# RWKV recurrence on one core: sixteen adaptive-norm row sums move from the turns of head pairs to the two draining turns and the state loop

## The reference

```
mod = silu(c) @ ada_w[i] + ada_b[i]                       # 6 * 1024 numbers
sh1, sc1, g1, sh2, sc2, g2 = split(mod)
h = rms(x) * (1 + sc1) + sh1
y = rwkv7_mix(h)          # scan over time: state = state * w + (state a) b + v k ; y = state r ; 16 heads of 64
x = x + g1 * y
h = rms(x) * (1 + sc2) + sh2                               # before the feed-forward
x = x + g2 * swiglu(h)
```

## Time and profile before

| | us |
|---|---|
| median of 3 runs | 2743.61 |
| lowest and highest run | 2742.07, 2745.13 |
| the profiled execution | 2749.12 |
| its span, first to last instruction | 2747.3 |
| PE busy in the span | 2567.3 (93%) |
| DVE busy in the span | 1184.1 (43%) |

### The profile page before, as it was taken

One profiled execution on the slowest core, in us unless ns is written; L12 is line 12 of the kernel. 1 busy time (PEld: TensorE's weight loads), 2 busy tenths in 40 slices (PEclk: granted clock), 3 DMA queues, 4 the chain that ended last, 5 costly groups with the idle time before them and its releaser, 6 DMA issues.

```text
span 2747.3 us, 33836 instructions
## 1 busy us (share of the span) xinstructions
PE 2567.3 (93%) x14040; PEld 1977.9 (72%) x14040; DVE 1184.1 (43%) x1813; ACT 978.5 (36%) x1441; POOL 977.9 (36%) x338
## 2 busy tenths in 40 slices
PE   7996667899999999999999999989899999999899
PEld 6745565388887878878887778969587777666586
DVE  4565884664444262442113352434306424444504
ACT  4652443432322243533232332222324334433423
POOL 2312320644444433453444444414433433222232
PEclk8997897899999999999999999999999999999999
DMA  6121343215555322122224332212122222111121
GB/s 263 62 77 42 91 91 118 79 69 191 193 188 199 138 92 77 47 77 77 92 94 171 133 126 92 95 42 95 39 92 86 87 88 96 62 48 61 39 92 62
DMA packets 92101, 272.11 MB, mean 99 GB/s; under 512 B 54720, under 2 KB 54848, under 8 KB 64320
## 3 DMA queue, kind: packets, MB, share of 16 engines
q1 hardware_dynamic: 89232, 255.03, 26.4%
q10 hardware_dynamic: 2736, 15.21, 1.4%
HBM read 264.44 MB, written 5.78 MB: 98 GB/s over the span
## 4 chain that ended last, share of the span: by engine, by line
PE 82%; DVE 8%; ACT 4%; issue 2%; DMA 2%; POOL 2%; SPq 0%; ACTq 0%; POOLq 0%; DVEq 0%
PE bank L348 20%; PE bank L350 20%; PE bank L349 20%; PE bank L284 2%; PE bank L283 2%; PE bank L282 2%; PE bank L2745 1%; PE bank L3279 1%; POOL ring_low L379 1%; PE bank L3257 1%; PE bank L2991 1%; DVE probs L3469 1%; ACT w_high L369 1%; PE bank L809 1%; PE bank L3261 1%
## 5 line engine op out<-in xcount | busy, mean ns | idle before, releaser
L379 POOL TENSOR_TENSOR ring_low<-ring,w_high 128x2048 fp32r<-128x2048 f32 (+2 forms) x184 | 803.3, 4367 | 1324.2 <-ACT w_high L369 1324.2
L348 PE MATMUL bank<-h_high,w_high 128*128 128x512 f32 (+1 forms) x1304 | 519.0, 398 | 7.5 <-POOL ring_low L379 3.6
L350 PE MATMUL bank<-h_high,ring_low 128*128 128x512 f32 (+1 forms) x1304 | 516.8, 396 | 0.0
L349 PE MATMUL bank<-h_low,w_high 128*128 128x512 f32 (+1 forms) x1304 | 513.7, 394 | 0.0
L369 ACT ACTIVATE w_high<-ring 128x2048 fp32r<-128x2048 f32 (+2 forms) x184 | 331.0, 1801 | 359.9 <-PE bank L350 341.2
L348 PEld LDWEIGHTS bank<-h_high,w_high 128*128 128x128 f32 (+1 forms) x1304 | 244.6, 188 | 70.1 <-issue 6.8
L349 PEld LDWEIGHTS bank<-h_low,w_high 128*128 128x128 f32 (+1 forms) x1304 | 244.3, 187 | 60.1 <-issue 0.7
L350 PEld LDWEIGHTS bank<-h_high,ring_low 128*128 128x128 f32 (+1 forms) x1304 | 244.4, 187 | 59.4
L348 PE MATMUL bank<-z_high,w_high 128*128 128x512 f32 x384 | 154.3, 402 | 6.1 <-DVE z_low L3476 2.7
L350 PE MATMUL bank<-z_high,ring_low 128*128 128x512 f32 x384 | 153.5, 400 | 0.0
L349 PE MATMUL bank<-z_low,w_high 128*128 128x512 f32 x384 | 153.0, 398 | 0.0
(11 more groups left out here) (451 smaller groups left out, 4436.2 us busy)
## 6 DMA issues: line engine op xcount, KB each, us to landing
ring<-in_stream SPq DMA_DIRECT2D x194, 1024.0 KB, 4.8
ada_slot<-in_ada_next SPq DMA_DIRECT2D x40, 512.0 KB, 3.3
ada_slot<-in_first SPq DMA_DIRECT2D x8, 1024.0 KB, 5.4
gain_weights<-in_gains ACTq DMA_DIRECT2D x4, 2048.0 KB, 12.2
scale_weights<-in_first SPq DMA_DIRECT2D x4, 1024.0 KB, 19.2
inverse<-scratch_inverse SPq DMA_DIRECT2D x16, 256.0 KB, 4.2
w_first<-in_first SPq DMA_DIRECT2D x2, 1024.0 KB, 8.1
x_res<-in_x SPq DMA_DIRECT2D x2, 1024.0 KB, 12.4
```

Source lines behind the costliest of these rows:

```text
L348: pe.matmul(out, w_high[:, k, cols], x_high, start=start, stop=False)
L349: pe.matmul(out, w_high[:, k, cols], x_low, start=False, stop=False)
L350: return pe.matmul(out, w_low[:, k, cols], x_high, start=False, stop=stop)
L379: pool.tensor_tensor(self.c.ring_low[:, b % SLOTS, 0:cols], self.c.ring[:, b % SLOTS, 0:cols], self.high_buf[:, b % 2, 0:cols].bitcast(F32 ...
```

## The change

`next_ada` leaves the 8 turns `0 <= p < KD`. The same eight calls now stand: `next_ada(0)` at the end of turn 8, `next_ada(1)` and `next_ada(2)` at the end of turn 9, and `next_ada(3)` to `next_ada(7)` in the steps c = 1 to 5 of the state loop, each behind the four state operations. SP issues the eight 1 MB loads no longer one a turn, but in a row behind the last of the four `g1` rows, each behind the sums of the one before. The loads of weight blocks for `rwkv_output` now wait for the last of the sums.

```
@@ vector, turns @@
-            if solves:
-                next_ada(p)
             if p == KD:
                 bonus_tile(1, 4)
                 g1_row(1)
...
                 bonus_tile(2, 0)
                 g1_row(2)
                 g1_row(3)
+                next_ada(0)
+            if p == KD + 1:
+                next_ada(1)
+                next_ada(2)
@@ vector, state loop @@
                 dve.tensor_tensor(part(new, g), part(Tm, g), decay_of(g, c), ALU.mult).then_inc(state.sem, 1)
+            if c <= 5:
+                next_ada(2 + c)
             if c == 1:
                 gated_tile(3, 4)
@@ sync, turn(p) @@
-            if p:
-                ada_sum.wait(sp, p - 1)
-            sp.dma_start(ada_slot[:, :], chip.io["first"][6 + p]).then_inc(ada_in.sem, 16)
@@ sync, behind the turns @@
         chip.load(sp, b_g)
-        ada_sum.wait(sp, KD - 1)
         for n in range(2):
             if n:
                 g1_sum.wait(sp, 1)
             sp.dma_start(g1_slot[:, :, :], chip.io["gains"][0, 0, 0, :, 2 * n:2 * n + 2, :]).then_inc(g1_in.sem, 16)
+        g1_sum.wait(sp, 3)
+        for n in range(KD):
+            if n:
+                ada_sum.wait(sp, n - 1)
+            sp.dma_start(ada_slot[:, :], chip.io["first"][6 + n]).then_inc(ada_in.sem, 16)
         y1_out.wait(sp, KD - 1)
-        g1_sum.wait(sp, 3)
+        ada_sum.wait(sp, KD - 1)
```

## The result

| | before | changed |
|---|---|---|
| median of 5 runs, us | 2745.13 | 2770.38 |
| lowest and highest, us | 2742.07, 2748.65 | 2763.83, 2776.43 |
| the profiled execution, us | 2749.12 | 2768.57 |
| its span, us | 2747.3 | 2766.8 |

The ratio is 1.0093, with a 95% interval of 1.0070 to 1.0115: the change costs 25.3 us by the medians. The forecast was 27.8 us and 2771.4.

The account below looks back on a forecast made before the run. PE, busy 93% of the span, was taken as the bound, so DVE changes count only where PE waits. Terms 28.8 + 1.5 + 0.5 - 3.0 = +27.8 us on 2743.6 gave 2771.4 us, range 2763 to 2780.

Parts of the forecast that it names:

- the ring of load and tiles: State loop: one load and two tiles alternate, 0.1 issue + 5.4 landing + 2.4 tiles = 7.9 us a step.
- the merge held up by the first load: Drain: DVE waits for load 0 and does two tiles ahead of the last y2 merge, which comes 8.0 us later.
- The turns, -3.0: Turns 0 to 7 without tiles and loads: 3.0 us given back, bounds 0 and 6.3.
- The drain, +16.3: From the last g1 row through three tile pairs: bonus_tile(3) starts at 500.7 instead of 484.36, 16.3 us later.
- rival 3: PE's clock falls in longer gaps: +9 us, 2780.5, in the loop; a part, +2.5, in the results part. Chance 12%.
- The loop, to +29.5 at the last state: State loop: with steps of 7.9 us the last state ends at 542.15 against 512.67, 29.5 us later.
- The landing term: In each loop step, the time a load takes to land after issue: 5.4 us.
- the tile term: In each loop step, the time of two tiles: 2.4 us, at 1.22 each.
- Meeting POOL, +1.5: Loop: only the first tile meets a POOL operation, 0.3 us for each of five steps; bounds 0 and 5.5.
- Weight blocks, +0.5: rwkv_output's weight blocks, issued after the last sums, arrive late: cost 0 to 2.2 us, taken as 0.5.
- POOL's backlog: End of the stage: with steps of 7.9 us POOL has no backlog and ends 0.73 us after ACT's last copy.
- Rivals 1, 2 and 4: Rival 1: turns return all work, 2744 (2%); 2: block_rows sooner, 2768 (17%); 4: loads 7.9 us each, 2789 (4%).

Follow-up runs that it names:

- e1: Changed kernel without the sixteen moved tiles and their eight loads (sums set to zero): 2740.13 us, ratio 0.9979 to the kernel before.
- e4: Half the change: pairs 0 to 4 stay in the turns, three pairs stand in the drain: 2760.94 us, ratio 1.0056 to the kernel before.
- e5: Other half: pairs 0 to 2 stay in the turns, five pairs stand in the state loop: 2761.35 us, ratio 1.0052 to the kernel before.
- e6: Kernel before, with tile pairs in turns 0, 1, 6, 7 and two pairs ahead of r_add in turns 8 and 9: 2747.88 us, ratio 1.0006.
- e2: Changed kernel with only the first of the eight moved loads, all tiles working on it: 2763.72 us, ratio 1.0062 to the kernel before.
- e3: Changed kernel with a second slot for the moved loads, loads 0 and 1 issued ahead: 2760.80 us, ratio 1.0050 to the kernel before.
- e7: Changed kernel plus twelve unread PE products ahead of each wait for the y2 merge: 2767.80 us, ratio 1.0086 to the kernel before.

## Why the prediction was right, by its steps

The mechanism was right: the ring of load and tiles, its length, the merge held up by the first load, and turns that give back little. That the sum came within 2.5 us also needed some luck. Several terms were off one way and others the other way.

- **The turns, -3.0.** Measured -5.2 (e1), within the bounds of 0 and 6.3; the interval of e1's ratio, 3.0 to 8.2, reaches beyond them. In the two traces turns 2 and 3 gave 1.2 each as worked out. Turns 1, 4 and 5 were wrong singly. Turn 1 gave 2.6 instead of 0. About 0.9 of it is DVE's first row, 0.15 us instead of 1.10: before, POOL was held up by the tiles of turn 0 and still at work when that row started, as POOL in order of time in the kernel before shows; in the changed kernel these four operations end at 275.96, before DVE's row at 276.45. In e4 and e5, which keep the tiles there, the row again takes 1.14 and 1.02 us.

```profile
272.07 4.36 POOL L1761 TENSOR_TENSOR level<-scores,const 64x512 f32<-64x512 f32 x2 [15.39 <-DVE scores L1658]
276.51 2.60 POOL L1761 TENSOR_TENSOR rw_all<-scores,const 64x512 f32<-64x512 f32 x2
```

  Most of the rest is PE's products between the mask and L1410, where L1290 took 1.97 us before and 1.09 after. The tiles did not decide that. The kernel before has L1290 at 1.97 us already at 251.30, ahead of its first tile; e5 and e6, with tiles there, show 1.09 in turn 1, and e2 and e3, without, 1.97. Where L1290 took 1.09 turn 1 lasted 20.8 us without tiles (changed kernel, e1, e7) and 22.0 to 22.1 with them; where it took 1.97, 23.0 and 23.1 without (e2, e3) and 23.4 and 23.7 with them (before, e4). So the tiles' part of the 2.6 us is 0.3 to 1.3, and the rest is the clock that these two executions happened to have, which is luck. The same holds for the 1.1 us of turn 8, where the two L1346 took 1.98 and 1.92 us before and 1.15 and 1.10 after.

  Turns 4 and 5 lost 1.6 each: turn 4 ends with 3.14 us of waiting for `block_rows`, and in turns 5 to 7 L1311 runs at the lower clock behind PE's longer waits. The prediction had the wait that replaces the tiles, but not that it can outlast them, nor that PE's clock can fall in it. Single executions differ in such turns, so only the sum from the medians is firm.

- **The drain, +16.3.** Measured +16.4, from two errors that cancel. The load took 4.8 us, not 5.4, so the merge came +7.3 and not +8.0. `r_add` came +8.7 (485.56 - 466.99 = 18.57, before 481.67 - 471.81 = 9.86), 1.4 more than the merge: behind a wait of 10.6 us PE's results part ran at the lower clock for longer than before (the two L1346 took 1.97 and 1.77 us, before 1.15 and 1.10). That is the part of rival 3, +2.5 by its pricing and 1.4 here. It does not come each time. In e2 and e4, behind the same wait of 10.6 us, the two took 1.15 and 1.10 and `r_add` stood 9.8 us behind the merge, as before; in e5, behind the wait of 3.3 us that the kernel before has there too, they took 1.98 and 1.89. Load 2 gave 0.6 back again.
- **The loop, to +29.5 at the last state.** Measured +29.9. The ring held: 8.05 us a step, forecast 7.9. The landing term was 0.6 too long and the tile term too short; a pair of tiles took 3.0 to 3.1 us in four of the five steps, 2.4 forecast.
- **Meeting POOL, +1.5.** Mis-sized: five pairs took 2.8, 3.0, 3.1, 3.1 and 3.1 us, 3.1 more than five times 2.4. The prediction had only the first tile of a pair meet a POOL operation. With the tiles starting earlier than forecast (0.2 to 0.9 us of idle time in front of them, not 1.4) both did: 1.42 to 1.54 us for the first in the last four steps and 1.73 for the second. This cost is in the +29.9, for which the prediction had 29.5 + 1.5 = 31.0; shorter loads made up for it.
- **PE's clock in the loop (rival 3).** It fell to a mean of 0.79, not to the lower level throughout, and PE did not become the bound: DVE's ring stayed longer than PE's work. Rival 3 was right that the clock falls and wrong on how far and on the price there.
- **Weight blocks, +0.5.** The size is near, the cause was wrong. ACT takes the first block 3.1 us behind the last state; before it was 516.31 - 512.67 = 3.6. It starts 1.0 us behind PE's first row of the next stage, before 0.9, so it is late by 0.1 us at most. PE is slower, because it stays at the lower clock for longer. Its clock is 0.50 at the start of the row in both kernels; before, it was at 0.95 in 518.4 to 519.8 already. PE in order of time, and the window of 540 to 544 us (columns as above):

```profile
539.80 5.49 PE L1885 MATMUL bank<-rw_all,const 128*128 128x512 f32 x6 [1.35 <-POOLq L3582]
```

```profile
540.00:544.00 4.00, 4.00 (x5) 1.60 (x6) 1.07 (x2) 2.52 (x2) 1.13 (x1) 0.50 1.01 422
```

These six took 4.38 us before: +1.1 in these two traces. That the change did it was not tested. POOL's backlog is gone as forecast; L1885 starts 2.1 us behind the last state, before 2.7.
- **Rivals 1, 2 and 4** fell. e1 prices the whole of the turns at 5 us. The rows' transfers did not quicken: the 9.4 us of turn 5 stand with no 1 MB load about, the 7.8 of before with one. The loads were quicker, not slower.

From the stage's first row on DVE to the reciprocal of `rwkv_output` the stretch is 26.4 us longer in these two traces (238.62 to 558.97, before 239.47 to 533.47). The spans differ by 19.5. Of the 6.9 us between, 0.9 lie ahead of the stage and the rest in later stages, none of which the change touches. The profiled execution of the kernel before took longer than any of its five runs in the table, that of the changed kernel 1.8 us less than its median. The medians of five differ by 25.3.

Open is why the rows of the later pairs come late. In the traces of the kernel before, the changed kernel and e1 the read-back of `block_rows` is issued 4.4 to 5.2 us behind the write for pairs 5 to 7 and 3.1 to 3.5 for the others, with and without 1 MB loads; in e7 pair 6 took 3.4. SP waits there for the writes, which in the changed kernel landed after 2.5 to 3.0 us in the earlier turns and after up to 4.5 in the later ones. For pair 5 the read itself took 4.3 us too. These landings limit what the turns can give.

## What to carry to other kernels

Price a move of work by what stands behind it at the new place, not by how busy the engine is there. DVE was idle for a third of the loop, but in slices of 1 us while it waited for PE or ACT, and two tiles of 3.1 us together turned DVE into its bound. A single buffer that is loaded only after use puts load and work in a ring: its length is the sum of both. Here a second buffer returned 12 of 25 us, and the work of the tiles kept the rest. Before counting work out of a full stream as gain, read what each wait behind it would be ended by: here 31 us removed gave 5.

## What the runs showed of the hardware

- PE's clock changes within single turns, and mostly where PE waits longer: the same 32 products took 1.96 us in 25 of 26 cases behind waits of 1.34 to 1.91 us, and 2.6 to 3.7 us in 21 of 22 cases behind waits of 1.98 to 5.0. A wait on PE can so cost up to 1.7 us more than its length. The wait just ahead does not settle it: 1.96 us behind 2.80 in e4, 3.54 behind 1.80 in e6.
- PE's clock in one and the same stretch differs between executions: ahead of the first tile, L1290 took 1.97 us in the traces of before, e5 and e6 and 1.09 in those of the changed kernel, e1 and e7. Turn 1 without tiles so lasted 20.8 us in three traces and 23.0 and 23.1 in two (e2, e3).
- A DVE tile with two SBUF inputs and a POOL addition take turns: 1.22 us becomes 1.73, and 0.72 becomes 1.71.
- Twelve fp32 products of 128x128 by 128x128 cost PE 2.94 us at full clock; they show as 24 records.
- A 1 MB load landed in 4.8 to 4.9 us alone and in 5.2 to 5.6 among the turns' small transfers.
